# A chunked RWKV-7 recurrence with turned results, group norm by matrix products, and the output product in the same stage

## The reference, cut to what matters

```python
def step(S, inp):                       # the recurrence, per token
    r_t, w_t, k_t, v_t, a_t, b_t = inp
    sa = einsum('bhvk,bhk->bhv', S, a_t)
    S = S * w_t[:, :, None, :] + sa[..., None] * b_t[:, :, None, :] + v_t[..., None] * k_t[:, :, None, :]
    y = einsum('bhvk,bhk->bhv', S, r_t)
    return S, y
...
mean = jnp.mean(y, axis=-1, keepdims=True)          # over the 64 channels of a head
var = jnp.mean(jnp.square(y - mean), axis=-1, keepdims=True)
y = (y - mean) * lax.rsqrt(var + GN_EPS) * gn_g + gn_b
y = y + jnp.sum(rh * kh * r_k, axis=-1, keepdims=True) * vh
out = (y.reshape(B, T, C) * g) @ wo
```

## Time and profile before

| | us |
|---|---|
| median of 3 runs (lowest, highest) | 1571.24 (1571.04, 1577.63) |
| the profiled execution | 1572.27 |
| its span in the trace | 1570.6 |
| PE busy | 1453.6 (93%) |
| DVE busy | 960.7 (61%) |
| ACT busy | 714.4 (45%) |

### The profile page before, as it was taken

The page is one execution under the profiler, slowest core; times in us unless marked ns, Lnnn a source line. Parts: engine busy times, 40 slices in busy tenths (PEclk is TensorE's granted clock), DMA queues, the critical chain, the costliest instruction groups (busy, mean ns, idle before and its releaser), DMA issues. The chain is left out here.

```text
span 1570.6 us, 28993 instructions
## 1 busy us (share of the span) xinstructions
PE 1453.6 (93%) x12780; PEld 1392.9 (89%) x12780; DVE 960.7 (61%) x1324; ACT 714.4 (45%) x1097; POOL 7.1 (0%) x12
## 2 busy tenths in 40 slices
PE   8999999997799999999979978958999995889999
PEld 8999999686699999999978977858999984789999
DVE  4656564346776446665579765357565678576565
ACT  5444454144564445444438424225444455354443
POOL 0000000000000000000000010000000000000000
PEclk9999999798899999999989988979999996899999
DMA  6555555151154334555514300023545430244552
GB/s 254 211 182 188 190 181 193 54 190 55 41 188 165 117 134 161 194 183 199 185 55 168 148 3 29 1 88 142 200 168 208 162 135 1 108 150 172 192 184 81
DMA packets 33093, 222.40 MB, mean 142 GB/s; under 512 B 3871, under 2 KB 5279, under 8 KB 6600
## 3 DMA queue, kind: packets, MB, share of 16 engines
q1 hardware_dynamic: 31912, 219.48, 39.2%
q10 hardware_dynamic: 1056, 1.07, 0.2%
HBM read 219.47 MB, written 1.06 MB: 140 GB/s over the span
## 5 line engine op out<-in xcount | busy, mean ns | idle before, releaser
L302 DVE TENSOR_TENSOR tile_lo<-ring,tile_hi 128x1024 fp32r<-128x1024 f32 x396 | 476.7, 1224 | 347.1 <-ACT tile_hi L292 346.2
L292 ACT ACTIVATE tile_hi<-ring 128x1024 fp32r<-128x1024 f32 x396 | 408.2, 1054 | 327.6 <-PE ps L344 303.3
L342 PE MATMUL ps<-hT_hi,tile_hi 128*128 128x256 f32 x1600 | 455.6, 285 | 9.9 <-DVE hidden_lo L751 7.6
L343 PE MATMUL ps<-hT_lo,tile_hi 128*128 128x256 f32 x1600 | 452.1, 283 | 0.0
L344 PE MATMUL ps<-hT_hi,tile_lo 128*128 128x256 f32 x1600 | 451.9, 282 | 0.0
L342 PEld LDWEIGHTS ps<-hT_hi,tile_hi 128*128 128x128 f32 x1600 | 305.7, 191 | 15.3 <-DVE hidden_lo L751 8.0
L343 PEld LDWEIGHTS ps<-hT_lo,tile_hi 128*128 128x128 f32 x1600 | 305.4, 191 | 0.0
L344 PEld LDWEIGHTS ps<-hT_hi,tile_lo 128*128 128x128 f32 x1600 | 305.2, 191 | 0.0
L344 PE MATMUL ps<-hidden_hi,tile_lo 128*128 128x256 f32 x864 | 243.2, 281 | 0.0
L342 PE MATMUL ps<-hidden_hi,tile_hi 128*128 128x256 f32 x864 | 243.1, 281 | 0.0
L343 PE MATMUL ps<-hidden_lo,tile_hi 128*128 128x256 f32 x864 | 243.0, 281 | 0.0
(11 more groups left out here) (469 smaller groups left out, 2296.1 us busy)
## 6 DMA issues: line engine op xcount, KB each, us to landing
ring<-stream SPq DMA_DIRECT2D x204, 1024.0 KB, 4.8
x_sb<-x SPq DMA_DIRECT2D x4, 256.0 KB, 3.9
bias<-f_dram ACTq DMA_DIRECT2D x1, 1024.0 KB, 8.4
squares<-mem SPq DMA_DIRECT2D x1, 1024.0 KB, 6.1
cum<-rows SPq DMA_DIRECT2D x1, 1024.0 KB
out<-x_sb SPq DMA_DIRECT2D x4, 256.0 KB, 2.2
const_sb<-const SPq DMA_DIRECT2D x1, 513.0 KB, 9.2
small_sb<-small SPq DMA_DIRECT2D x1, 485.5 KB, 9.0
```

The source lines that it names most:

```text
L292: act.activation(e.w_hi[:, n % SPLIT, :], e.ring[:, tile % RING, span(n % 2, HALF)], ACT.Copy).then_inc(e.tile_hi.handle, 1)
L302: dve.tensor_tensor(e.w_lo[:, n % SPLIT, :], e.ring[:, CUT[n // 2] % RING, span(n % 2, HALF)], e.w_hi[:, n % SPLIT, :].bitcast(F32), ALU.s ...
L342: pe.matmul(out, left[0], right[0], start=start, stop=False)
L343: pe.matmul(out, left[0], right[1], start=False, stop=False)
```

## The change

The steps, the group norm and the output product become one stage, `rwkv_tail`, with no barrier between them. In `right_side` and `solve` each head computes its 64 columns alone, and the state's product 128 columns instead of 256. In `finish` the operands are exchanged: the result has channels on partitions, each head in its own half, so a product has weights of 64 columns and streams 128. The state's two products share bank 6 with `y`.

The group norm works on `y` with channels on partitions, in four units of two pairs. `centre` multiplies by identity minus the head's mean (a new constant), ScalarE writes squares and the centred copy, `sums` adds squares per head, `variance`, `square_root` and `inverse` work on 64 rows for two units at a time, `spreads` spreads the inverse root back, and `norm` is three passes of 128x512. The shift and bonus are turned (`turn`), multiplied by the gate during the steps, and the gain is multiplied into the gate; so gain and shift are columns of `small_sb`, and the DMA of rows is gone. The first units are centred, summed and spread in rounds 10 to 17, the others between the products with `wo`, which now take half a tile at a time and wait for the unit that they read. VectorE's rests of the two half tiles move from before the steps to after its step 9; bonus to step 0. The evacuations copy whole 128 columns; the state is written after `y` is done. In ScalarE's order `centre(0)` and `centre(1)` stand after the copy of `y` in rounds 11 and 12, and in round 18 that copy is followed by `heads(0)`. The indentation is cut by eight.

```diff
-    rwkv_halves(e, w)
-y = e.pair(stack, "y_gated", [P, KC, SEQ])
-rwkv_group_norm(e, w, y)
-out_stage(e, "wo", y, [("ln_mlp0", e.hT)])
...
-    with nc.Block() as block, ExitStack() as stack:
+    centre_bank, spread_bank = (7, 7, 0, 1), (7, 7, 3, 0)
...
-    lo, hi = ROWS_AT["gn_g"][0], ROWS_AT["gn_b"][1]
-    sp.dma_start(flat(w.cum), e.a.rows[:, lo:hi]).then_inc(*loaded.one(16))
-    sp.wait_ge(*loaded.at(16))
+    feed(e, sp, g0 + 4)
...
-            pe.matmul(pairs(4), w.AR[:, pair, t, 0, :], state(pair), start=True, stop=False)
+            pe.matmul(e.ps[:, 4, 0:P], w.AR[:, pair, t, 0, :], Z[:, pair, :], start=True, stop=False)
         for par in range(2):
-            mm = pe.matmul(wide(4, par), grams[:, n % GRAMS, par, 0, :], values(n),
-                           start=not t, stop=not t or par == 1)
+            mm = pe.matmul(e.ps[:, 4, head(par)], grams[:, n % GRAMS, par, 0, :], values(n)[:, head(par)],
+                           start=not t and par == 0, stop=par == 1)
         mm.then_inc(*w_done.one())
...
     def finish(n):
         t, pair = place(n)
         pe.wait_ge(*u_copied.at(n + 1))
-        if not t:
-            if pair >= 1:
-                pe.wait_ge(*z_copied.at(pair))
-            pe.matmul(e.ps[:, 7, 0:P], v.k_nat[:, span(pair, P)], values(n), start=True, stop=False)
-            mm = pe.matmul(e.ps[:, 7, 0:P], v.b_nat[:, span(pair, P)], u[:, both(n)], start=False, stop=True)
-            mm.then_inc(*z_done.one())
         if n >= 1:
             pe.wait_ge(*y_copied.at(n))
-        if t:
-            pe.matmul(pairs(6), w.AR[:, pair, t, 1, :], state(pair), start=True, stop=False)
-        for par in range(2):
-            pe.matmul(wide(6, par), grams[:, n % GRAMS, par, 1, :], values(n), start=not t, stop=False)
-            mm = pe.matmul(wide(6, par), grams[:, n % GRAMS, par, 2, :], u[:, both(n)], start=False,
-                           stop=not t or par == 1)
+        if not t:
+            pe.matmul(e.ps[:, 6, P:2 * P], v.k_nat[:, span(pair, P)], values(n), start=True, stop=False)
+            pe.matmul(e.ps[:, 6, P:2 * P], v.b_nat[:, span(pair, P)], u[:, both(n)], start=False, stop=True)
+        else:
+            pe.matmul(e.ps[:, 6, 0:P], Z[:, pair, :], w.AR[:, pair, t, 1, :], start=True, stop=False)
+        for part, left in ((1, values(n)), (2, u[:, both(n)])):
+            for par in range(2):
+                mm = pe.matmul(e.ps[head(par), 6, 0:P], left[:, head(par)], grams[:, n % GRAMS, par, part, :],
+                               start=not t and part == 1, stop=part == 2)
         mm.then_inc(*y_done.one())
...
+    def turn(b):
+        pe.wait_ge(*boosted.at(1))
+        if b >= 1:
+            pe.wait_ge(*given_ready.at(b))
+        for i in range(2):
+            for t in range(TT):
+                tr = pe.transpose(e.ps[:, 7, span(2 * i + t, P)], boost[:, t, span(2 * b + i, P)], const(e, "ident"))
+        tr.then_inc(*turned.one())
+    def centre(h):
+        pe.wait_ge(*y_copied.at((5, 7, 13, 15)[h] + 1))
+        if h == 0:
+            pe.wait_ge(*given_ready.at(4))
+        elif h == 1:
+            pe.wait_ge(*centred.at(1))
+        else:
+            pe.wait_ge(*gram_kept.at(15))
+        for i in range(2):
+            mm = pe.matmul(e.ps[:, centre_bank[h], span(i, SEQ)], const(e, "centre"), y[:, 2 * h + i, :],
+                           start=True, stop=True)
+        mm.then_inc(*centre_done.one())
+    def sums(group):
+        pe.wait_ge(*centred.at(2 * group + 2))
+        if group:
+            pe.wait_ge(*gram_kept.at(16))
+        for j in range(2):
+            for i in range(2):
+                mm = pe.matmul(e.ps[quarter(2 * group + i), (7, 2)[group], 0:SEQ], head_sum[:, j, :],
+                               squares[:, 2 * i + j, :], start=j == 0, stop=j == 1)
+        mm.then_inc(*summed.one())
+    def spreads(h):
+        pe.wait_ge(*inv_ready.at(h // 2 + 1))
+        if h == 1:
+            pe.wait_ge(*normed.at(1))
+        for j in range(2):
+            mm = pe.matmul(e.ps[:, spread_bank[h], span(j, SEQ)], head_back[quarter(h), j, :], inv[quarter(h), 1, :],
+                           start=True, stop=True)
+        mm.then_inc(*spread.one())
     for n in range(N + 3):
         if n < N:
...
             solve(n - 2)
         if 0 <= n - 3:
             finish(n - 3)
+        if 3 <= n < 7:
+            turn(n - 3)
+        if n in (10, 11):
+            centre(n - 10)
+        if n == 13:
+            sums(0)
+        if n in (16, 17):
+            spreads(n - 16)
+        if n == 17:
+            centre(2)
+    centre(3)
+    mark_tail(e)
+    def half_tile(i, k):
+        if k == 0:
+            pe.wait_ge(*split.at(i + 1))
+        wt = arrived(e, pe, g0 + i, k)
+        for m in range(KC):
+            mm = product(pe, e.ps[:, 4 + m // 2, span(m % 2, SEQ)], cut(wt, ALL, span(m, P)),
+                         cut(dst, ALL, 2 * i + k, ALL), i == 0 and k == 0 and m % 2 == 0, False)
+        mm.then_inc(*e.tile_done.one())
+    half_tile(0, 0)
+    sums(1)
+    half_tile(0, 1)
+    half_tile(1, 0)
+    spreads(2)
+    pe.wait_ge(*centred.at(3))
+    spreads(3)
+    half_tile(1, 1)
+    half_tile(2, 0)
+    half_tile(2, 1)
+    pe.wait_ge(*split.at(4))
+    row_to_T(e, pe, g0 + 3, dst, 6, False, True)
...
+    def centre(h):
+        act.wait_ge(*centre_done.at(h + 1))
+        if h == 0:
+            act.wait_ge(*turned.at(4))
+        if h == 2:
+            act.wait_ge(*summed.at(1))
+        src = e.ps[:, centre_bank[h], :]
+        act.activation(squares[:, two(h % 2), :].rearrange("p m n -> p (m n)"), src, ACT.Square)
+        copy(y[:, two(h), :].rearrange("p m n -> p (m n)"), src).then_inc(*centred.one())
+    def square_root(group):
+        rows = span(group, 2 * BLK)
+        act.wait_ge(*var_ready.at(group + 1))
+        act.activation(inv[rows, 0, :], inv[rows, 0, :], ACT.Sqrt).then_inc(*root.one())
+    def heads(h):
+        act.wait_ge(*normed.at(h + 1))
+        copy(dst[0][:, two(h), :], y[:, two(h), :]).then_inc(*headed.one())
+    heads_after(e, act, 2 * g0)
...
+        if n in (11, 12):
+            centre(n - 11)
+        if n == 15:
+            square_root(0)
+        if n == 18:
+            heads(0)
+    centre(2)
+    heads(1)
+    centre(3)
+    heads_after(e, act, 2 * g0 + 1)
+    square_root(1)
+    heads_after(e, act, 2 * g0 + 3)
+    heads(2)
+    heads(3)
+    heads_after(e, act, 2 * (g0 + 3))
+    tail_scalar(e, act, outs, then=lambda: heads_after(e, act, 2 * (g0 + 4)))
...
+    def variance(group):
+        rows = span(group, 2 * BLK)
+        dve.wait_ge(*summed.at(group + 1))
+        dve.tensor_scalar(inv[rows, 0, :], e.ps[rows, (7, 2)[group], 0:SEQ], 1.0 / HD, GN_EPS, ALU.mult,
+                          ALU.add).then_inc(*var_ready.one())
+    def inverse(group):
+        rows = span(group, 2 * BLK)
+        dve.wait_ge(*root.at(group + 1))
+        dve.reciprocal(inv[rows, 1, :], inv[rows, 0, :]).then_inc(*inv_ready.one())
+    def norm(h):
+        part = y[:, two(h), :].rearrange("p m n -> p (m n)")
+        dve.wait_ge(*centred.at(h + 1))
+        dve.wait_ge(*spread.at(h + 1))
+        link.done(dve.tensor_tensor(part, part, e.ps[:, spread_bank[h], :], ALU.mult))
+        link.done(dve.tensor_tensor(y[:, two(h), :], y[:, two(h), :], gate[:, two(h), :], ALU.mult))
+        dve.tensor_tensor(y[:, two(h), :], y[:, two(h), :], given[:, two(h), :], ALU.add).then_inc(*normed.one())
+    def rests(h):
+        dve.wait_ge(*headed.at(h + 1))
+        dve.tensor_tensor(dst[1][:, two(h), :], y[:, two(h), :], dst[0][:, two(h), :].bitcast(F32),
+                          ALU.subtract).then_inc(*split.one())
     for n in range(N):
...
+        if n == 0:
+            dve.tensor_tensor(flat(w.ep).rearrange("p (h d) -> p h d", d=HD), heads_of_v(w),
+                              w.bonus[:, :, :].rearrange("p t h -> p (t h)").unsqueeze(2).to_broadcast([P, TT * RH, HD]),
+                              ALU.mult).then_inc(*boosted.one())
+        if 4 <= n < 8:
+            dve.wait_ge(*turned.at(n - 3))
+            for i in range(2):
+                pair = 2 * (n - 4) + i
+                x = dve.scalar_tensor_tensor(out=given[:, pair, :], in0=e.ps[:, 7, span(i, SEQ)],
+                                             scalar=small(e, "gn_b")[:, pair:pair + 1], in1=gate[:, pair, :],
+                                             op0=ALU.add, op1=ALU.mult)
+            x.then_inc(*given_ready.one())
+        if n == 8:
+            dve.wait_ge(*given_ready.at(4))
+            link.done(dve.tensor_tensor(gate[:, :, :], gate[:, :, :], small(e, "gn_g").unsqueeze(2).to_broadcast(
+                [P, KC, SEQ]), ALU.mult))
+        if n == 9:
+            rests_after(e, dve, 2 * g0)
...
+        if n == 14:
+            variance(0)
+        if n == 15:
+            inverse(0)
+    norm(0)
+    norm(1)
+    rests(0)
+    rests(1)
+    rests_after(e, dve, 2 * g0 + 1)
+    variance(1)
+    inverse(1)
```

(44 more changed lines are left out.)

100 lines of the change are left out of this document (19 added, 81 removed).

## The result

| | before | after |
|---|---|---|
| median (lowest, highest) of 4 runs, us | 1571.14 (1570.23, 1577.63) | 1549.11 (1543.63, 1555.02) |
| profiled execution, us | 1572.27 | 1552.4 |
| its span | 1570.6 | 1551.1 |

The ratio is 0.9839 [0.9814, 0.9863]: faster by 25 us (22 to 29), where 16 had been forecast, with 1555 for the time and 1548 to 1562 for the range. The median of after alone lies just inside that range; by the ratio the time is 1546, just outside it.

The account below looks back on a forecast made before the run. TensorE sets the recurrence's pace, then a 23.0 us group-norm hole. Products with wo start 19.4 us earlier but take 3.4 longer: 1572.3 - 16.0 = 1556.3, a profiled execution 1.0 above the median, so 1555; range 1548 to 1562.

Parts of the forecast that it names:

- The failed step: Tail and mlp1, behind the output product: same order as before, nothing more won or lost; larger constants cost under 0.4 us.
- The stage's term: Merged stage: last product with wo at 1050.9 against 1066.9, 16.0 us less (19.4 - 3.4).
- The prediction's own sign of being wrong: It called itself wrong if the stage ended less than 12 us earlier, or more than 20.
- The steps give nothing back: Recurrence rounds before round 16: savings of 7.6 us against 7.5 of added work, so round 16 begins as before.
- Pairs in `finish`: Every step's `finish`: 64-column products overlap in pairs, 0.6 us from first pair to next gram, saving 0.30 per step.
- second rival: Pairs in the steps' `finish` don't overlap: 1.0 us to the next gram, 5.6 us lost over 13 rounds, 1561; chance 0.11.
- first rival: `right_side` and `solve`: 64 moving columns cost half, 0.055 per record, 5.6 us more gained, 1549.5; chance 0.12.
- round 11's wait: `centre(1)` needs bank 7 emptied by ScalarE behind the copy of y: 2.3 us of idle TensorE.
- End of the loop: Round 16 to the first product with wo: waits of 0.6 and 1.0; that product at 1022.3, 19.4 us earlier.
- Output product: Products with wo, sums and spreads between them: 28.6 us against 25.2 before, including a 2.8 wait before half tile (2,0).
- The clock at 1.00 from round 2 to mlp1: Expected sign of the forecast: TensorE keeps its full clock through the whole stage.
- The fourth rival: Rounds 3 to 18: TensorE falls to half clock, 50 us of work takes 50 more, 1605, slower than before; chance 0.03.

Follow-up runs that it names:

- tile_moved: Kernel before with split weight tiles and the constants behind them 64 bytes per partition higher, all else unchanged modulo 256 bytes; run once for its trace, no single time given.
- unpaired: Kernel after with the order in `finish` changed, so that one head's two products precede the other head's; run once for its trace, 1548.74 us.
- placed_reordered: Kernel after with hT and hidden 192 bytes above the weights, plus three stage-order edits (spreads together, `centre` earlier, `norm(2)`/`rests(2)` earlier): 1526.08 us, ratio 0.9699.

## Why the prediction was wrong

**The failed step.** "The tail and mlp1 follow in the same order as before ...: nothing more is won or lost." The order was the same, the places weren't. I costed the grown tables as a DMA (under 0.4 us) and not as a shift of everything allocated behind them. That term, put at nothing, measured 10 us (6 to 13) with the shift alone: `hidden` went from 128 to 192 bytes above the weights, o_parts and y_turned from 0 to 64; o_swa lost, from 192 to 0 (119.9).

**The stage's term**, 16.0 forecast to the last product with wo, was too large: 11.3 in the first pair of traces, 10.7 in the second, and 13 (9 to 17) by the ratio with the layout put back. The prediction's own sign of being wrong, a stage that ends less than 12 us earlier, is met, counted from the stage's first gram. The two errors have opposite signs and cancel in part, 10 us missing outside the stage and 3 to 5 too many in it; that the median of after still came inside the range is luck. By its steps:

- The steps at 16 rounds: forecast 53.7 us to round 16's start. Measured 55.9 (953.55 to 1009.48), of which the 6.8 us at 0.50 cost 3.4: 52.5 at full clock. "The steps give nothing back" holds. Pairs in `finish` 0.59 (0.6 forecast; second rival out), 0.11 per 64-column record (no saving; first rival out), round 11's wait 2.10 (2.3 forecast).
- End of the loop: waits 0.47 and 0.94 (0.6 and 1.0 forecast). First wo product 69.3 us after the first gram (64.6 forecast); the two stretches at 0.50, nearly all work, cost 6.2 to 6.8, so 62.5 to 63.1 at full clock.
- Output product: a wait of 3.17 before half tile (2,0) (2.8). From its first product to its last, start to start, it took 28.45, with 28.6 forecast to its end. `spreads(2)` and `(3)`, on different row groups, took 1.07 together (1032.63 to the next product) and not 2.0. The last product came 97.7 after the first gram (93).
- "The clock at 1.00 from round 2 to mlp1" is wrong, and it is the largest miss in the stage: the 13.7 us at 0.50 cost 6.2 to 6.8, and the last product came 4.7 late against the forecast. The fourth rival had the mechanism, at 0.03 and with 50 us of work at the lower level. What brings such stretches on stays open. Every kernel with the merged stage showed some (13.6 to 23.9 us), except the reordered one.

## What to carry to other kernels

A table that grows moves every later tensor; compare operand addresses before giving the gain to the edit. Where products run back to back, read their spacing by operand, scan the distance from weights to moving operand in 32-byte steps, and place by it: 27 us here, for pads. Judge an edit in the stage against a partner with the same addresses, and set the clock's share apart first: after a wait of 2.1 us was removed by itself, the stage was 0.3 us shorter, with 6.8 us more at the lower clock.

## What the runs showed of the hardware

- A fast product of 128x128 weights on 256 columns takes 113.3 to 120.0 ns, and which values occur goes by the byte distance of its two operands modulo 256, with 0 and 96 the worst and 64 and 192 the best. The Trainium skill, "TensorE: Matmul & The Clock Gate", Step-by-step: what each phase is for, says that loading the next weights takes no SBUF read bandwidth from the running matmul, through a port of its own. `tile_moved` speaks against it: moving only the weights took y_gated from 119.9 to 113.6 and hT from 117.4 to 120.0. That the two reads collide is the plain reading, but only the distance is shown.
- Products in different halves of 64 columns start out of the order in which the kernel has them (`unpaired`; 0.59 and 0.60 us for eight records in the two orders).
- Four records of 32 rows from one row group and four from another ran as long as four (1.21 for the eight in `placed_reordered`, 1.13 for four).
